# First FFN: one plain group instead of two in front of the groups of seven block products

## The chip, the cores and the metric

The kernel runs on one core of one Trainium2 chip. The metric is the device time of one execution in microseconds (us). Three runs of the kernel before gave 3054.82, 3054.83 and 3055.84 us, a median of 3054.83. The profiler's engines are PE (TensorE matmuls), PEld (TensorE's weight loads), DVE (VectorE), ACT (ScalarE), POOL (GpSimd) and SP (SyncE, which here only issues DMAs).

## The reference

The reference is a whole model on 512 rows of 1024 features: two layers of FFN, mixer, cross-attention and a second FFN, and then a hybrid block with an FFN of its own. Only the first operation of the first layer matters here:

```
def swiglu_ffn(x, w_gu, w_down):
    gate, up = jnp.split(x @ w_gu, 2, axis=-1)
    return (jax.nn.silu(gate) * up) @ w_down

x = x + 0.5 * swiglu_ffn(rms_norm(x, ffn1_norm[0]), ffn1_w_gu[0], ffn1_w_down[0])
```

The weight w_gu is 1024 x 5632 (gate and up of 2816 columns each), and everything is float32.

## The kernel before

Every float32 product is made of three matmuls on a split into an upper and a lower part: an operand `raw` becomes `wh` (rounded by ACT, line 100) and `wl` (the rest, subtracted by DVE, line 103), and TensorE adds wh·h, wl·h and wh·l (line 94). Weights stream from memory through four tiles `raw` (SP issues the loads), and each half megabyte of them is split by one ACT instruction of 128x1024 and then one DVE instruction of 128x1024. TensorE needs the lower part, so it waits for DVE.

The gate and up projection of an FFN is made in 11 groups of 256 gate columns and 256 up columns. There are two ways to make a group:

- **Plain.** Four chunks of 256 rows of the weight, for each of them 24 matmuls with 512 moving columns: 96 matmuls. Its inputs are the normed and split x (`hTh`, `hTl`), chunk by chunk.
- **Seven block products** (a fast matrix product: the weights and x are cut into two by two blocks). Seven times 24 matmuls with 256 moving columns: 168 matmuls. The seven blocks of weights have the names ge, s2, s1, s3, go, s4 and uo, in that order. Five of them are loads of half a megabyte by SP. s1 and s3 become sums while a second DMA, issued by POOL, adds to the tile; s2 and s4 are sums that DVE makes in a tile `u_raw`. On x's side the products need four sums of x's blocks, X1 to X4, each split into `u_Xnh` and `u_Xnl`.

The table `PLAIN` (line 246) says how many plain groups stand in front. In the last of them the sums of x are made ("builds" in `act_fast_up` and `dve_fast_up`). ACT multiplies x by the norm's gain into B, eight instructions of 128x512 on the tile `u_F` (`act_gained`). DVE combines blocks of B to X1, X2, X3 and X4 (`dve_combine`, four instructions of 128x1024). ACT rounds each of them to its upper part (`act_upper_x`), and DVE subtracts that for the lower part (`dve_lower_x`). The weights of the first group of seven are split by the same two engines, in program order among these:

```
                if builds and kp == 2:
                    dve_combine(dve, f, 4)
                    for i in X_ORDER[:2]:
                        dve_lower_x(dve, f, i)
                elif builds and kp == 3:
                    dve_split(dve, n + 4)
```

Here `dve_split(dve, n + 4)` makes the lower part of block ge, the first that TensorE needs of the group of seven; ahead of it DVE adds ge and s1 to s2 (`dve_lower_block`). ACT has the same order in `act_fast_up`: gains, upper X2 and X1, upper ge, upper X3 and X4, then the copy of the row scales (`u_R`).

In the first FFN ("f1u0" for its gate and up, line 860 for TensorE) the first plain group runs while x itself still arrives: TensorE transposes x between its matmuls, ACT and DVE split the transposed x straight out of the accumulator and copy it to `xT` (`act_start`, `dve_start`), ACT makes the row sums of squares, and POOL raises them to the power of -1/2 (`rc`, line 103). In the other four FFNs the plain groups start from an x that lies finished. POOL's own queue holds that power first and then the adding DMAs of s1 and s3 (`pool_fast_up`). All order is written out by hand: each engine works off its list, and a wait in the list holds what stands behind it.

Of the kernel before, what the change touches and what calls it, by code (L numbers as in the profile page):

```python
# [242 lines left out]
    return G  # L243


PLAIN = {"f1u0": 2, "f2u0": 1, "f1u1": 1, "f2u1": 1, "f3u": 2}
HALF = S // 2
BESIDE = {"in0": "out0", "in1": "out1", "gb": "yb"}

# [18 lines left out]
def program(nc, T, out):  # L268
# [80 lines left out]
    def fast(name, g):  # L349

        return g >= PLAIN.get(name, g + 1)

# [34 lines left out]
    def enter(e, key):  # L387
        for who in ("pe", "act", "dve", "pool"):
            e.wait_ge(ended, (key, who))
# [17 lines left out]
    def slot_of(name, g, what):  # L407

        r, odd = begin[name, PLAIN[name] - 1] % NRAW, (g - PLAIN[name]) % 2 == 0
        if what == "s1":  # L410
            return (raw[r], raw_in[r], s1_sum[0]) if odd else (more[0], more_in[0], s1_sum[1])
        if what == "s3":
            return (raw[(r + 2) % NRAW], raw_in[(r + 2) % NRAW], s3_sum[0]) if odd else (more[1], more_in[1], s3_sum[1])
        if what == "ge":
            return raw[(r + 1) % NRAW], raw_in[(r + 1) % NRAW], None
        if what == "go":
            return raw[(r + 3) % NRAW], raw_in[(r + 3) % NRAW], None
        return more[2], more_in[2], None
# [29 lines left out]
    def sp_weights(sp):  # L448
# [12 lines left out]
        for n, entry in enumerate(stream):  # L461
# [3 lines left out]
            if len(entry) == 3:  # L465
# [3 lines left out]
                for j, what, src in ((2, "s1", "ue"), (0, "ge", "ge"), (3, "s3", "ue"), (4, "go", "go"), (6, "uo", "uo")):  # L469
                    if (g, what) == (PLAIN[name], "uo"):  # L470
                        enter(sp, name)
# [53 lines left out]
    def dve_lower_block(dve, n):  # L525
        name, g, i = stream[n]
        block_ready(dve, name, g, i)
        if BLOCKS[i] == "ge":
            block_ready(dve, name, g, 2)
            s1 = slot_of(name, g, "s1")[0]  # L530
            if g > PLAIN[name]:
                dve.wait_ge(w_lo, n - 2)
# [1014 lines left out]
    class Ffn:  # L1547
        def __init__(self, up, down):
            self.up, self.down = up, down
            self.F, self.sg, self.R = Act(Fh, Fl, S, ("F", up)), u_sg, u_R  # L1550
            self.plain = PLAIN[up]

# [1795 lines left out]
```

How the kernel before makes its waits and increments, by code:

```python
    def wait_ge(self, flag, key):  # L75
        if self.e is None:
            return
        sem, value, who, place = flag.at[key]
        if who is not None:
            if self.seen.get(who, 0) >= place:
                return
            self.seen[who] = place
        else:
            if self.seen.get(sem, 0) >= value:
                return
            self.seen[sem] = value
        self.e.wait_ge(sem, value)
# [299 lines left out]
    def enter(e, key):  # L387
        for who in ("pe", "act", "dve", "pool"):
            e.wait_ge(ended, (key, who))
# [58 lines left out]
    def sp_weights(sp):  # L448
        sp.dma_start(x_rows[:, :, 0:256], x_in_rows[:, :, 0:256]).then_inc(x_in[0], 0, 16)
        first_weights(sp, 1)
        sp.dma_start(x_rows[:, :, 256:512], x_in_rows[:, :, 256:512]).then_inc(x_in[1], 0, 16)
        sp.wait_ge(x_in[0], 0)
        held = {}
        def load(tile, parts, flag_, key):
            for f_, k_ in held.get(tile, ()):
                sp.wait_ge(f_, k_)
            for dst, src in parts:
                sp.dma_start(dst, src).then_inc(flag_, key, 16)
# [31 lines left out]
    def act_first(act, kk):  # L491
        key = 0 if kk else "half"
        act.wait_ge(raw_in[0], key)
        act.activation(wh[0][:, kk, 0:chunk(0)], raw[0][:, kk, 0:chunk(0)], AF.Copy).then_inc(w_hi, key)
        act.split = 1
# [1 line left out]
    def dve_first(dve, kk):  # L497
        key = 0 if kk else "half"
        dve.wait_ge(raw_in[0], key)
        dve.wait_ge(w_hi, key)
# [248 lines left out]
    def act_square(act, N, src, c):  # L749
        act.wait_ge(x_ready, (src, c))
        if c >= 2:
```

## Time and profile before

| what | value |
|---|---|
| median of the runs | 3054.83 us |
| the profiled execution | 3054.1 us, its span 3052.4 us |
| TensorE busy | 3037.4 us, 17960 matmuls |
| VectorE busy | 2036.1 us |
| ScalarE busy | 1416.4 us |
| GpSimd busy | 450.5 us |
| mean granted TensorE clock | 0.999 |

A busy TensorE is a chain of pipelined matmuls: what one costs is read from the distance of two starts, not from its own duration. A granted clock of 1.00 is the level of 2.4 GHz and 0.50 that of 1.2 GHz. The first FFN's two plain groups stand before 55.11 us in the trace, its nine groups of seven behind that.

### The profile page before, as it was taken

How to read it: one execution, taken by the hardware profiler on the slowest of the kernel's cores; microseconds unless marked ns; L12 is line 12 of the kernel's file. 1: busy time of each engine (PE TensorE's matmuls, PEld its weight loads, DVE VectorE, ACT ScalarE, POOL GpSimd, SP SyncE). 2: the span in 40 equal slices, each digit the busy share in tenths (PEclk: the TensorE clock that was granted, in tenths of full speed). 3: DMA queues.
4: the chain of work that ended last, by engine and by line, in shares of the span. 5: the costliest groups of instructions: out<-in, count | busy, mean ns of one | idle time of the engine just before them, and what ended most of it. 6: DMA issues, size and time to landing. Idle time of an engine off the chain costs nothing.

```text
span 3052.4 us, 44801 instructions
## 1 busy us (share of the span) xinstructions
PE 3037.4 (100%) x17960; PEld 2620.2 (86%) x17960; DVE 2036.1 (67%) x2896; ACT 1416.4 (46%) x2189; POOL 450.5 (15%) x550
## 2 busy tenths in 40 slices
PE   9999999999999999999999999999999999999999
PEld 8998886887999899988867879998887786789987
DVE  7886258755888478863565657886336876578873
ACT  5444247544444244442455545444236727454442
POOL 1112014212110021100310212110153200031100
PEclk9999999999999999999999999999999999999999
DMA  7762330423874267633232416763332231247732
GB/s 209 176 165 98 103 97 29 148 67 99 198 176 136 97 160 176 166 107 104 83 99 75 152 49 165 177 167 106 89 96 83 82 105 35 76 111 190 170 117 70
DMA packets 287360, 366.93 MB, mean 120 GB/s; under 512 B 12304, under 2 KB 211344, under 8 KB 287024
## 3 DMA queue, kind: packets, MB, share of 16 engines
q1 hardware_dynamic: 233392, 304.42, 31.5%
q0 software_dynamic: 53184, 59.32, 12.0%
q8 instruction: 142, 2.33, 0.3%
q14 instruction: 66, 0.54, 0.1%
q10 hardware_dynamic: 576, 0.33, 0.0%
HBM read 361.92 MB, written 2.10 MB: 119 GB/s over the span
## 4 chain that ended last, share of the span: by engine, by line
PE 94%; issue 3%; DVE 2%; POOL 1%; ACT 0%; DMA 0%; POOLq 0%; ACTq 0%; DVEq 0%
PE ps L94 91%; PE ps L97 3%; POOL evQ L142 1%; DVE wl L103 0%; POOL evPb L142 0%; POOL evPa L142 0%; DVE hTl L109 0%; DMA misc<-in_misc 0%; DVE xT L103 0%; DVE u_X2l L103 0%; DVE u_raw L103 0%; DVE u_X3l L103 0%; DVE u_X4l L103 0%; DVE evQ L115 0%; DVE s_gb L103 0%
## 5 line engine op out<-in xcount | busy, mean ns | idle before, releaser
L103 DVE TENSOR_TENSOR wl<-raw,wh 128x1024 fp32r<-128x1024 f32 (+2 forms) x485 | 597.0, 1237 | 499.1 <-ACT wh L100 494.9
L100 ACT ACTIVATE wh<-raw 128x1024 fp32r<-128x1024 f32 (+2 forms) x485 | 505.1, 1049 | 810.9 <-PE ps L94 770.0
L94 PE MATMUL ps<-hTh,wh 128*128 128x256 f32 (+1 forms) x2016 | 671.0, 333 | 0.7 <-ACT hTh L100 0.7
L94 PE MATMUL ps<-hTh,wl 128*128 128x256 f32 (+1 forms) x2016 | 666.6, 331 | 0.0
L94 PE MATMUL ps<-hTl,wh 128*128 128x256 f32 (+1 forms) x2016 | 624.0, 330 | 0.2 <-DVE hTl L109 0.2
L94 PEld LDWEIGHTS ps<-hTh,wh 128*128 128x128 f32 x2016 | 383.9, 190 | 42.1 <-issue 9.2
L94 PEld LDWEIGHTS ps<-hTh,wl 128*128 128x128 f32 x2016 | 383.7, 190 | 37.7 <-issue 7.1
L94 PEld LDWEIGHTS ps<-hTl,wh 128*128 128x128 f32 x2016 | 382.1, 190 | 37.4 <-issue 4.7
L100 ACT ACTIVATE wh<-u_raw 128x1024 fp32r<-128x1024 f32 x190 | 201.4, 1062 | 297.8 <-PE ps L94 281.9
L94 PE MATMUL ps<-u_Fh,wl 128*128 128x512 f32 x704 | 273.9, 389 | 0.0
L94 PE MATMUL ps<-u_Fh,wh 128*128 128x512 f32 x704 | 273.9, 389 | 0.0
L103 DVE TENSOR_TENSOR wl<-u_raw,wh 128x1024 fp32r<-128x1024 f32 x190 | 232.2, 1222 | 40.1 <-ACT wh L100 39.7
L103 POOL TENSOR_TENSOR xn<-xn 128x512 f32<-128x512 f32 x69 | 100.1, 1450 | 988.8 <-ACT xn L100 751.4
L94 PE MATMUL ps<-u_Fl,wh 128*128 128x512 f32 x704 | 232.9, 389 | 0.0
L94 PE MATMUL ps<-wh,hTh 128*128 128x512 f32 (+2 forms) x576 | 216.8, 377 | 0.0
L94 PE MATMUL ps<-wl,hTh 128*128 128x512 f32 (+2 forms) x576 | 215.1, 374 | 0.0
L94 PE MATMUL ps<-wh,hTl 128*128 128x512 f32 (+2 forms) x576 | 195.1, 374 | 0.0
L94 PEld LDWEIGHTS ps<-u_Fl,wh 128*128 128x128 f32 x704 | 132.1, 188 | 27.5
L94 PEld LDWEIGHTS ps<-u_Fh,wl 128*128 128x128 f32 x704 | 132.2, 188 | 27.3
L94 PEld LDWEIGHTS ps<-u_Fh,wh 128*128 128x128 f32 x704 | 132.1, 188 | 27.3
L94 PEld LDWEIGHTS ps<-wh,hTh 128*128 128x128 f32 x576 | 108.3, 188 | 20.1 <-issue 2.2
L94 PEld LDWEIGHTS ps<-wl,hTh 128*128 128x128 f32 x576 | 108.4, 188 | 19.2 <-issue 1.4
(423 smaller groups left out, 6106.6 us busy)
## 6 DMA issues: line engine op xcount, KB each, us to landing
raw<-in_ffn_w_gu SPq DMA_DIRECT2D x118, 512.0 KB, 4.6
raw<-in_ffn_w_down SPq DMA_DIRECT2D x88, 512.0 KB, 3.6
u_raw<-in_ffn_w_gu SPq DMA_DIRECT2D x77, 512.0 KB, 4.9
raw<-in_ffn_w_gu POOLq DMA_DIRECT2D x40, 512.0 KB, 6.1
u_raw<-in_ffn_w_gu POOLq DMA_DIRECT2D x38, 512.0 KB, 6.1
raw<-in_xa_w_kv SPq DMA_DIRECT2D x32, 512.0 KB, 3.6
raw<-in_w_in SPq DMA_DIRECT2D x28, 512.0 KB, 3.6
raw<-in_od_w_in SPq DMA_DIRECT2D x24, 512.0 KB, 3.8
```

What stands on the lines that cost most here:

```text
L94: return self.made(lambda e: e.matmul(*a, **k))
L97: return self.made(lambda e: e.transpose(*a, **k))
L100: return self.made(lambda e: e.activation(*a, **k))
L103: return self.made(lambda e: e.tensor_tensor(*a, **k))
L142: return self.made(lambda e: e.affine_select(*a, **k))
```

## The change

One number: the first FFN gets one plain group, and then ten groups of seven.

```
-PLAIN = {"f1u0": 2, "f2u0": 1, "f1u1": 1, "f2u1": 1, "f3u": 2}
+PLAIN = {"f1u0": 1, "f2u0": 1, "f1u1": 1, "f2u1": 1, "f3u": 2}
```

So x's sums are made in the program's first group. On VectorE, right behind the split of the last plain chunk of that first group (`wl<-raw,wh` behind `rc<-stat`), stood before:

```order
L106 TENSOR_SCALAR rc<-stat 128x4
L103 TENSOR_TENSOR wl<-raw,wh 128x1024 x5
L103 TENSOR_TENSOR u_sg_63<-ps,u_R 128x512
L103 TENSOR_TENSOR u_sg_64<-ps,u_R 128x512
L103 TENSOR_TENSOR u_F<-ps,u_R 128x512 x2
L103 TENSOR_TENSOR u_F<-u_F 128x1024 x3
L103 TENSOR_TENSOR u_F<-u_F,u_sg_63 128x512
L103 TENSOR_TENSOR u_F<-u_F,u_sg_64 128x512
L103 TENSOR_TENSOR u_F<-u_F 128x1024
L103 TENSOR_TENSOR u_X2l<-u_F,u_X2h 128x1024
L103 TENSOR_TENSOR u_X1l<-u_F,u_X1h 128x1024
```

And now at the same place (`u_F<-u_F` are the four sums X1 to X4, `u_raw_60<-raw` is the weight sum s2, and the `wl` behind it is block ge):

```order
L106 TENSOR_SCALAR rc<-stat 128x4
L103 TENSOR_TENSOR wl<-raw,wh 128x1024
L103 TENSOR_TENSOR u_F<-u_F 128x1024 x4
L103 TENSOR_TENSOR u_X2l<-u_F,u_X2h 128x1024
L103 TENSOR_TENSOR u_X1l<-u_F,u_X1h 128x1024
L103 TENSOR_TENSOR u_raw_60<-raw 128x1024
L103 TENSOR_TENSOR wl<-raw,wh 128x1024
L103 TENSOR_TENSOR u_X3l<-u_F,u_X3h 128x1024
L103 TENSOR_TENSOR u_X4l<-u_F,u_X4h 128x1024
L103 TENSOR_TENSOR wl<-u_raw_60,wh 128x1024
```

Four splits of plain chunks are gone from between; the order from the sums of x to the split of ge is as it was.

On ScalarE, behind the copies of x (`xT<-ps`), stood before:

```order
L100 ACTIVATE xT<-ps 128x512 x4
L100 ACTIVATE wh<-raw 128x1024 x3
L100 ACTIVATE u_R<-ps 128x512
L100 ACTIVATE wh<-raw 128x1024
L100 ACTIVATE u_F<-xT,prm 128x512 x8
L100 ACT_TABLE_LOAD
```

And now:

```order
L100 ACTIVATE xT<-ps 128x512 x4
L100 ACTIVATE u_F<-xT,prm 128x512 x8
L100 ACTIVATE u_X2h<-u_F 128x1024
L100 ACTIVATE u_X1h<-u_F 128x1024
L100 ACTIVATE wh<-raw 128x1024
L100 ACTIVATE u_X3h<-u_F 128x1024
L100 ACTIVATE u_X4h<-u_F 128x1024
L100 ACTIVATE u_R<-ps 128x512
```

The eight gains follow the copies of x directly, and the copy of the row scales comes behind the upper parts of the sums.

## Rows read from the trace of the kernel before

**Rows 1.** The page: span, TensorE's busy time, the chain that ended last.

```profile
span 3052.4 us, 44801 instructions
PE 3037.4 (100%) x17960; PEld 2620.2 (86%) x17960; DVE 2036.1 (67%) x2896; ACT 1416.4 (46%) x2189; POOL 450.5 (15%) x550
...
PE 94%; issue 3%; DVE 2%; POOL 1%; ACT 0%; DMA 0%; POOLq 0%; ACTq 0%; DVEq 0%
```

**Rows 2.** Waits of TensorE over the span: us in total, times, longest.

```profile
PE ps L94 <- ACT evQ L100: 3.7, 3, 2.2
PE ps L94 <- POOL rc L103: 1.2, 1, 1.2
```

**Rows 3.** Windows: the second plain group, the first group of seven.

```profile
core 0: us, PE busy (x) PEld busy (x) DVE busy (x) ACT busy (x) POOL busy (x), PEclk, DMA share, GB/s
33.24:55.11 21.87, 21.87 (x99) 18.10 (x98) 19.74 (x21) 15.76 (x20) 3.51 (x3) 1.00 0.88 201
55.11:75.27 20.16, 20.16 (x170) 20.15 (x169) 16.77 (x19) 9.48 (x11) 2.55 (x2) 1.00 0.75 194
```

**Rows 4.** Timeline of PE: start, us, what; end of the first plain group.

```profile
32.43 1.05 PE L94 MATMUL ps<-misc,rc 128*128 128x128 f32 x8
33.24 0.48 PE L94 MATMUL ps<-hTh,wh 128*128 128x512 f32 x1
...
75.27 0.28 PE L94 MATMUL ps<-hTh,wh 128*128 128x256 f32 x1
75.39 0.28 PE L94 MATMUL ps<-hTh,wl 128*128 128x256 f32 x1
```

**Rows 5.** Timeline of ACT: copies of x, plain splits, gains, upper parts.

```profile
24.61 2.04 ACT L100 ACTIVATE xT<-ps 128x512 f32<-128x512 f32 x4
26.51 2.97 ACT L100 ACTIVATE wh<-raw 128x1024 fp32r<-128x1024 f32 x3
33.60 0.60 ACT L100 ACTIVATE u_R<-ps 128x512 f32<-128x512 f32 x1 [4.11 <-PE ps L94]
...
35.04 5.01 ACT L100 ACTIVATE u_F<-xT,prm 128x512 f32<-128x512 f32 x8
...
42.42 1.04 ACT L100 ACTIVATE u_X2h<-u_F 128x1024 fp32r<-128x1024 f32 x1
```

**Rows 6.** Timeline of DVE: last split of group one, sums, block ge.

```profile
24.80 1.22 DVE L103 TENSOR_TENSOR wl<-raw,wh 128x1024 fp32r<-128x1024 f32 x1 [0.85 <-ACT wh L100]
...
45.85 1.22 DVE L103 TENSOR_TENSOR u_X1l<-u_F,u_X1h 128x1024 fp32r<-128x1024 f32 x1
46.98 1.22 DVE L103 TENSOR_TENSOR u_raw<-raw 128x1024 f32<-128x1024 f32 x1
48.12 1.22 DVE L103 TENSOR_TENSOR wl<-raw,wh 128x1024 fp32r<-128x1024 f32 x1
...
53.79 1.28 DVE L103 TENSOR_TENSOR u_sg<-ps,u_R 128x512 f32<-128x512 f32 x2
```

**Rows 7.** Timeline of POOL, and landings of its two first adding DMAs.

```profile
24.11 1.02 POOL L103 TENSOR_TENSOR rc<-rc,half 128x4 f32<-128x4 f32 x1 [23.06 <-DVE rc L106]
...
raw<-in_ffn_w_gu POOLq DMA_DIRECT2D x1, 512.0 KB, 7.6
...
raw<-in_ffn_w_gu POOLq DMA_DIRECT2D x1, 512.0 KB, 10.3
```

**Rows 8.** Windows around TensorE's longest pause: PEclk is the granted clock.

```profile
482.75:484.75 2.00, 0.00 (x0) 0.00 (x0) 0.14 (x1) 2.00 (x6) 0.55 (x2) 1.00 0.00 0
...
485.50:485.75 0.25, 0.25 (x4) 0.13 (x2) 0.00 (x0) 0.25 (x1) 0.00 (x0) 0.55 0.00 0
485.75:488.50 2.75, 2.75 (x13) 1.85 (x9) 2.31 (x2) 2.56 (x8) 1.17 (x1) 0.50 0.00 0
...
488.75:489.00 0.25, 0.25 (x2) 0.25 (x4) 0.25 (x1) 0.25 (x2) 0.25 (x1) 0.62 0.68 49
489.00:490.00 1.00, 1.00 (x7) 0.53 (x6) 0.81 (x2) 0.55 (x3) 1.00 (x3) 1.00 0.79 305
```

**Rows 9.** Timeline of PE behind that pause, at the lower clock.

```profile
484.86 1.46 PE L94 MATMUL ps<-e_kbT,e_qbT 64*128 64x384 f32 x8 [2.17 <-ACT evQ L100]
...
487.59 0.63 PE L94 MATMUL ps<-hTh,wl 128*128 128x512 f32 x1
488.01 0.63 PE L94 MATMUL ps<-hTh,wh 128*128 128x512 f32 x1
```

**Rows 10.** Windows at the program's end, where TensorE stops.

```profile
3046.00:3047.00 1.00, 0.94 (x5) 0.44 (x3) 1.00 (x2) 0.03 (x1) 0.00 (x0) 1.00 0.08 27
...
3049.00:3050.00 1.00, 0.00 (x0) 0.00 (x0) 0.93 (x2) 0.00 (x0) 0.00 (x0) 0.50 0.00 0
```

## The prediction

> **What bounds the kernel now.** I read the page first, then the waits of TensorE, then the windows and the engines' timelines from 20 to 80 us. On the page TensorE is busy in 3037.4 of 3052.4 us and makes up 94% of the chain that ended last [rows 1]. Its longest wait in the whole span is 2.2 us [rows 2]. So the time is the sum of what TensorE does, and each us in which it is made to wait is a us of the result, unless it was waiting later anyway. DVE is the second engine: it is busy for 19.74 of the 21.87 us of the second plain group, where x's sums are made, and for 16.77 of 20.16 us in a group of seven [rows 3].
>
> **What goes: TensorE's work.** The second plain group runs from 33.24 to 55.11 us, which is 21.87 us; a group of seven runs from 55.11 to 75.27 us, which is 20.16 us [rows 3]. Neither holds a gap. One plain group less and one group of seven more takes 21.87 - 20.16 = 1.71 us away, if the new group can start at 33.24 us, where the transposed scales of the first group are done and the next group begins now [rows 4]. At both bounds this term is the same, since both durations stand in the trace.
>
> **What the new group waits for.** Its first product needs x itself, which is long split, and the lower part of block ge. DVE comes to that split only behind the sums, and these wait for ACT's eight gains.
>
> - ACT ends its copies of x at 24.61 + 2.04 = 26.65 us [rows 5]. What follows now, three plain splits, is gone, so the gains start there. They take 5.01 us for eight, the last ends at about 31.7 us. The gains can't go earlier: the copies they read end at 26.65, and ACT has no idle time in front.
> - DVE has split the last plain chunk at 24.80 + 1.22 = 26.0 us [rows 6] and then waits for B. X1 needs only the first four gains (about 29.2 us) and is out of the way. X2 needs the last gain and starts at 31.75.
> - From X2 to the lower part of ge DVE has seven instructions of 128x1024 in a row: X2, X3, X4, the lower X2, the lower X1, the sum s2, and ge's lower part. Such instructions start 1.14 us apart and the last takes 1.22 us [rows 6], so 6 x 1.14 + 1.22 = 8.06 us: ge is ready at 39.8 us. ACT's upper X2 and X1 (1.04 us each [rows 5], from about 33.0) and upper ge are done by 36 us, ahead of DVE.
> - TensorE therefore stands from 33.24 to 39.8 us: a new wait of **6.55 us**. The second plain group was the cover for this chain; now nothing but the first group's end stands beside it.
>
> Bounds of this term: if X2 waited for nothing and the gains were free, DVE would still need 8.06 us from 26.0 us for the seven and 1.14 for X1, and ge would be ready at 35.2 us, a wait of 2.0 us. If all of DVE's instructions took the 1.22 us of a single one [rows 6], it is 7.1 us. I take 6.55, which follows the order as it stands.
>
> **The second wait.** Behind ge DVE has the lower X3, the lower X4 and s2's lower part: 3 x 1.14 us more, done at 43.2 us. Block ge's product of 24 matmuls takes 24 x 0.12 = 2.88 us (starts 0.12 us apart [rows 4]) and ends at 42.7. So 0.5 us more are lost. From there DVE is ahead: s1 at 44.3, s3 at 46.7 (with two evictions of 0.6 us [rows 6] in between), against starts of TensorE at 46.1 and 49.0; uo at 55.0 against 57.6. At TensorE's next group it is 2.5 us ahead, and behind that the pattern is the one of now.
>
> **What stands at nothing.** SP issues five loads of 512 KB in place of eight of 256 KB, and POOL two adding DMAs more, 1.5 MB in all. SP's first two (s1, ge) go out when the tiles of the first chunks come free, at the same places as the plain loads now. POOL's s1 stands behind the power, which ends at 24.11 + 1.02 = 25.1 us; the two first adding DMAs landed 7.6 and 10.3 us after issue [rows 7], so s1 lands at 32.7 to 35.4 us, and DVE asks for it with s2's sum at 37.4. It is hidden by two to five us, but only by the wait itself: each us that the chain of sums lost would bring it nearer. The copy of the row scales, now behind ACT's upper parts, falls to about 38 us, and its first reader on DVE is at 44.3. The last group of seven gets one multiplication of 128x1024 by the row scales more on DVE, about 1.2 us, inside the 20.16 - 16.77 = 3.4 us that DVE has free there [rows 3]; without that cover it would be 1.2 us.
>
> **The clock.** In the row TensorE stood still from 482.75 to 484.75 us, and from 485.5 to 488.8 us the granted clock was 0.50, the 1.2 GHz level, though TensorE was working again [rows 8]. At the end of the program it stops within 3046 to 3047 us and the clock is at 0.50 by 3049 [rows 10]. A pause of 6.55 us is over three times the one and longer than the other, so I expect the clock to be at 0.50 when the new group starts. Two matmuls of 512 columns lay 0.42 us apart at the lower level [rows 9], so 256 columns lie about 0.21 apart by halving, against 0.12 now. If the low stretch again lasts 3.3 us, it costs 3.3 x (1 - 0.12 / 0.21) = 1.4 us. It falls into block ge's product, behind which TensorE would have waited 0.5 us anyway, so 0.9 us remain. Bounds: 0 if the clock is back in time, and a stretch twice as long costs 2.8 - 0.5 = 2.3 us.
>
> The Trainium skill has the rule for this on "TensorE: Matmul & The Clock Gate", section "What's actually happening": the throttled state is the default, and only activity lifts it. By that rule the pause is paid twice, as a wait and as slow matmuls behind it, and the sum below is 6.3 us; without it 5.4 us. The stretch at 0.50 in the trace agrees with it.
>
> **The sum.** 6.55 + 0.5 + 0.9 - 1.71 = +6.3 us, rounded. Against the profiled execution of 3054.1 us that is 3060.4. The median of the runs shown lies 0.7 above that execution, so a median of the changed kernel should be near 3054.8 + 6.3 = 3061.1 us. TensorE is the chain's owner all the way behind, so I see nothing that pays it back.
>
> **Rivals.**
>
> - *The clock holds.* The pause is paid once: 6.55 + 0.5 - 1.71 = 5.4 us, 3060.2. For it: in the trace the clock fell only 0.7 us after TensorE had started again (484.86 us [rows 9]), so when it falls and when it comes back is not fixed to the pause. Against it: both pauses of the trace led to 0.50. Chance 0.15.
> - *The low clock lasts twice as long*, or a term of the chain grows as much (an adding DMA of s1 beyond its 10.3 us by over 2 us): 5.4 + 2.3 = 7.7 us, 3062.5. For it: nothing in the trace says how soon the clock comes back behind a longer pause, and there is one stretch alone to measure by. Chance 0.14.
> - *The time comes back later.* The other engines gain 6 us of lead while TensorE stands, and waits like the 3.7 us on evQ [rows 2] shrink: 6.3 - 3.7 = 2.6 us, 3057.4. Against it: that wait is for ACT's work on what TensorE has just made, so it moves along. Chance 0.05.
> - *Faster.* The sums of x stay covered: TensorE starts the new group at 33.24 us, or before 33.24 + 1.71 = 34.95, from which on it is a loss. Then the gain of 1.71 us is left, 3053.1. The place is DVE's split of ge: it would have to be done 4.8 us earlier than worked out. That takes gains that run beside x's copies, or a split of ge ahead of the sums, and the written order has neither. Chance 0.03.
>
> **How the numbers follow.** The forecast, +5.8 to +7.0 us with its own range of 3060 to 3062, has a chance of 0.63. About 0.2% (6.1 us) is what a measurement of this kernel can tell from no change, and the forecast lies on that line: of its 0.63 I give 0.40 to the upper side and 0.23 to the lower. Slower by over 0.2%: 0.40 + 0.14 = 0.54, and 0.01 of the clock's rival by the spread of the runs: 0.55. Within 0.2%: 0.23 + 0.14 + 0.05 = 0.42. Faster: 0.03. The range takes in the first two rivals with the runs' spread: from 3054.1 + 4.9 = 3059.0 to 3054.8 + 8.2 = 3063.0.
>
> **What would show it.** In the profile after: TensorE's last row of the first group at about 33.2 us, and its first matmul of 256 columns at 39.8, with the wait put down to DVE's wl. The four `u_F<-u_F` rows of DVE from 29 to 35 us, and ge's wl ending at 39.8. PEclk at 0.50 in some 3 us from about 39 us on, and the first 24 matmuls of 256 columns 0.2 us apart for a while. TensorE's second group of seven beginning at about 61.4 us in place of 55.11, and from there the same distance to the end. The prediction is wrong if 256-column matmuls start before 35 us, if ge's split on DVE stands in front of the sums, or if the distance at 61 us is not the one at the end.

## The result, and the profile after

The changed kernel takes 3061.22 us (median of 14 runs, 3060.80 to 3062.89) against 3054.90 us (14 runs, 3054.29 to 3056.79): 6.3 us more, a ratio of 1.0021 with a 95% interval of 1.0014 to 1.0029. The forecast was 3061.1. The profiled execution took 3062.45 us, 1.2 us over its median, and that of the kernel before 3054.1 us, 0.8 us under its own; so the two profiles lie 8.3 us apart, more than the medians.

The page of the changed kernel, for [rows 1]:

```profile
span 3060.7 us, 44966 instructions
PE 3038.6 (99%) x18032; PEld 2625.0 (86%) x18032; DVE 2045.7 (67%) x2905; ACT 1420.8 (46%) x2193; POOL 452.5 (15%) x552
```

TensorE has 72 matmuls more (168 - 96) and is busy for only 1.2 us more, although the span grew by 8.3 us. The difference is waiting, and the waits of TensorE name it at once (total, times, longest). Of [rows 2] nothing grew by more than 0.3 us; one row is new, with a wait of 6.1 us in the first group and one of 0.44 us far behind, at 1117.49 us, to which I come back:

```profile
PE ps L94 <- DVE wl L103: 6.5, 2, 6.1
PE ps L94 <- ACT evQ L100: 4.0, 4, 2.2
PE ps L94 <- POOL rc L103: 1.2, 1, 1.2
```

Timeline of PE at the end of the first group, which answers to [rows 4]: start, us, what, and the idle time in front with its releaser. From the second fence line on the matmuls are those of the new group of seven.

```profile
32.99 1.05 PE L94 MATMUL ps<-misc,rc 128*128 128x128 f32 x8
40.13 0.58 PE L94 MATMUL ps<-hTh,wh 128*128 128x256 f32 x1 [6.09 <-DVE wl L103]
40.51 0.41 PE L94 MATMUL ps<-hTh,wl 128*128 128x256 f32 x1
40.73 0.41 PE L94 MATMUL ps<-hTl,wh 128*128 128x256 f32 x1
...
45.42 0.32 PE L94 MATMUL ps<-u_X2h,wh 128*128 128x256 f32 x1
...
46.05 0.28 PE L94 MATMUL ps<-u_X2l,wh 128*128 128x256 f32 x1
46.17 0.28 PE L94 MATMUL ps<-u_X2h,wh 128*128 128x256 f32 x1
...
62.72 0.28 PE L94 MATMUL ps<-hTh,wh 128*128 128x256 f32 x1
```

Block ge's 24 matmuls start 0.21 us apart (5.29 us in all), block s2's 0.12 us apart, and the next group begins at 62.72 us. The first group itself began some 0.5 us later in this profile than in that of before; it does so in every later profile but four, three of which are of the changed kernel itself (32.43 to 32.51 us), so it is no part of the change. From here on I measure from the transposition of the scales (the row of `misc,rc`): to the next group it was 55.11 - 32.43 = 22.68 us before and is 62.72 - 32.99 = 29.73 us now.

The two engines behind the wait, first ACT, then DVE (for [rows 5] and [rows 6]):

```profile
24.92 2.04 ACT L100 ACTIVATE xT<-ps 128x512 f32<-128x512 f32 x4
26.99 5.02 ACT L100 ACTIVATE u_F<-xT,prm 128x512 f32<-128x512 f32 x8
```

```profile
25.11 1.23 DVE L103 TENSOR_TENSOR wl<-raw,wh 128x1024 fp32r<-128x1024 f32 x1 [0.85 <-ACT wh L100]
29.68 1.23 DVE L103 TENSOR_TENSOR u_F<-u_F 128x1024 f32<-128x1024 f32 x1 [3.35 <-ACT u_F L100]
32.04 3.50 DVE L103 TENSOR_TENSOR u_F<-u_F 128x1024 f32<-128x1024 f32 x3 [1.13 <-ACT u_F L100]
35.46 1.22 DVE L103 TENSOR_TENSOR u_X2l<-u_F,u_X2h 128x1024 fp32r<-128x1024 f32 x1
36.59 1.22 DVE L103 TENSOR_TENSOR u_X1l<-u_F,u_X1h 128x1024 fp32r<-128x1024 f32 x1
37.73 1.22 DVE L103 TENSOR_TENSOR u_raw<-raw 128x1024 f32<-128x1024 f32 x1
38.86 1.22 DVE L103 TENSOR_TENSOR wl<-raw,wh 128x1024 fp32r<-128x1024 f32 x1
```

Read it from below: ge's lower part ends at 38.86 + 1.22 = 40.08 us and TensorE starts at 40.13. Above it DVE goes without a gap back to 32.04, and there it waited 1.13 us for ACT's last gain; in front of X1 it had waited 3.35 us for the first gains.

The clock (windows; the third last number is the granted clock, the columns are those of [rows 3]), for [rows 8]: 0.50 is already there in the pause, and for all of block ge.

```profile
33.80:38.50 4.70, 0.24 (x3) 0.05 (x1) 4.70 (x5) 4.70 (x6) 0.00 (x0) 1.00 1.16 255
39.00:40.13 1.13, 0.00 (x0) 0.00 (x0) 1.13 (x2) 1.13 (x2) 0.45 (x1) 0.50 0.00 1
40.13:45.42 5.29, 5.29 (x25) 5.29 (x25) 5.29 (x6) 3.25 (x4) 0.83 (x1) 0.50 0.77 164
45.50:62.72 17.22, 17.22 (x145) 17.22 (x145) 16.71 (x20) 8.25 (x10) 2.55 (x2) 1.00 0.84 222
```

### The profile page after: what moved, and what is told of

It reads as the page before. It is cut to its first block, busy times and chain, and to the rows that moved or that the text cites. A ratio compares the mean times of both kernels' runs of the same rounds, so it can differ in the third digit from the quotient of the medians.

```text
span 3060.7 us, 44966 instructions
## 1 busy us (share of the span) xinstructions
PE 3038.6 (99%) x18032; PEld 2625.0 (86%) x18032; DVE 2045.7 (67%) x2905; ACT 1420.8 (46%) x2193; POOL 452.5 (15%) x552
## 4 chain that ended last, share of the span: by engine, by line
PE 93%; issue 3%; DVE 2%; POOL 1%; ACT 1%; DMA 0%; POOLq 0%; ACTq 0%; DVEq 0%
PE ps L94 90%; PE ps L97 3%; POOL evQ L142 0%; DVE wl L103 0%; POOL evPb L142 0%; DVE u_F L103 0%; DMA misc<-in_misc 0%; ACT u_F L100 0%; DVE u_raw L103 0%; DVE u_X2l L103 0%; DVE hTl L109 0%; POOL evPa L142 0%; DVE xT L103 0%; DVE u_X4l L103 0%; DVE u_X3l L103 0%
```

## The experiments

Each kernel was compared with the kernel before on the same chip; medians of before in these comparisons were 3054.85 to 3055.02 us (for x9_look and x10_look there is one run of before, 3053.57 us).

**1. TensorE kept busy in the pause (x1_warm).** Added to the changed kernel, behind the first plain group:

```
...
+            if (g, kp) == (0, None):
+                b = home["f1u0", 1] + 1
+                pe.wait_ge(drained, pe.held[b])
+                pe_warm(pe, b, 30)
```

> The changed kernel with 30 dummy products of 128 columns (on the constant `ones`, into an accumulator bank that is free) behind the first plain group, so that TensorE works through the new wait instead of standing. Theory: the wait for DVE stays (first matmul of 256 columns at 39.8 to 40.1 us), but the granted clock stays at 1.00; block ge takes 2.9 us in place of 5.3, 0.5 us of wait for s2 come back, and the group of seven from its first matmul to the next group's takes about 20.7 us in place of 22.6. Time 3060.2 us, 1 to 2 us under the changed kernel. Rival, that the slow block is not the pause's doing but that of DVE's lower parts coming late: the group still takes 22.6 us and the time stays at 3061.2.

Measured: 3060.36 us (11 runs, 3059.95 to 3061.25). Windows of the dummy products and of the group of seven:

```profile
34.10:40.70 6.60, 6.60 (x62) 6.60 (x61) 6.60 (x7) 6.25 (x8) 0.92 (x1) 1.00 0.85 191
40.72:61.16 20.44, 20.44 (x172) 20.29 (x170) 20.41 (x24) 11.11 (x13) 1.61 (x2) 1.00 0.83 198
```

The clock stays at 1.00, the group takes 20.44 us in place of 62.72 - 40.13 = 22.59, and with the dummies it lasts 27.95 us from the transposition to the next group. The dummies ran 0.4 us beyond what was needed (ge was ready at 40.3). So the pause has a price of its own for the wait, and a second one for the clock. On the way to the next group, the overrun included, the second is 29.73 - 27.95 = 1.8 us against the result's profile and 1.0 to 1.2 us against the two shorter profiles of experiment 7. In the medians it is 0.9 us: nine of these eleven runs lie under the lowest of the changed kernel's, 3060.80 us.

**2. The sums without the gains (x2_nogain).** The first FFN's sums are taken from x; the eight gains and the wait for them are gone, so the norm's gain is missing in the sums.

```
...
-            return Bf[:, 4 * k:4 * k + 4, HALF * t:HALF * t + HALF]
+            return (xT if f.up == "f1u0" else Bf)[:, 4 * k:4 * k + 4, HALF * t:HALF * t + HALF]
...
```

> The changed kernel without the eight gains of the first FFN: x's sums are taken from x itself (the norm's gain is left out of the sums). Theory: the sums start when x's last copy is there, 27.0 us in place of 32.0, and ge is ready after eight DVE instructions, 36.2 to 36.6 us; s2's sum asks for s1's adding DMA at about 33.8, which lands at about 34.2. TensorE's wait falls from 6.3 to about 2.5 us, and the time to about 3057 us with the clock at 1.00 and 3058 if it still falls. Rival, that the gains run beside what DVE would wait for anyway (s1's sum): the wait stays above 5 us, the time above 3060.

Measured: 3056.90 us (11 runs, 3056.06 to 3059.45); the profiled execution took 3057.79 us. DVE and PE:

```profile
27.34 1.23 DVE L103 TENSOR_TENSOR u_F<-xT 128x1024 f32<-128x1024 f32 x1 [0.70 <-ACT xT L100]
...
35.53 1.22 DVE L103 TENSOR_TENSOR wl<-raw,wh 128x1024 fp32r<-128x1024 f32 x1
...
36.80 0.39 PE L94 MATMUL ps<-hTh,wh 128*128 128x256 f32 x1 [2.49 <-DVE wl L103]
```

The wait falls from 6.09 to 2.49 us. So the gains are 3.6 us of it, and the other 2.5 us are DVE's eight instructions. In the profiled execution the clock still fell, but late (windows behind the restart); its mean over the span is 0.999 there, while six of the other ten runs, the median among them, show 1.000.

```profile
36.80:38.00 1.20, 1.20 (x10) 1.20 (x11) 1.20 (x2) 0.85 (x1) 0.00 (x0) 1.00 1.19 242
38.50:41.50 3.00, 3.00 (x16) 3.00 (x16) 3.00 (x4) 2.34 (x2) 1.28 (x1) 0.50 1.07 367
42.00:43.00 1.00, 1.00 (x11) 1.00 (x10) 1.00 (x2) 1.00 (x2) 0.21 (x1) 1.00 0.99 110
```

**3. Block ge's split first (x4_ge_first).** The changed kernel with another order only. DVE's list (ACT's follows it; X4 goes into the group of seven):

```
...
+                    dve_combine(dve, f, 1)
+                    dve_combine(dve, f, 2)
+                    dve_split(dve, n + 4)      # ge
+                    dve_lower_x(dve, f, 2)
+                    dve_first_sum(dve)         # s2's sum
+                    dve_lower_x(dve, f, 1)
+                    dve_split(dve, n + 5)      # s2
+                    dve_split(dve, n + 6)      # s1
+                    dve_combine(dve, f, 3)
+                    dve_split(dve, n + 7)      # s3
+                    dve_lower_x(dve, f, 3)
...
```

> The changed kernel with another order in its first group: ACT rounds block ge right behind the gains, DVE makes ge's lower part right behind X2 and then each lower part when TensorE needs it (X2, s2's sum, X1, s2, s1, X3, s3, X3; X4 only in the group of seven). Nothing is added or left out. Theory that the place of ge's split makes the wait, and DVE's amount of work the rest: ge is ready at 34.4 us and the first wait is 0.6 us, but DVE is busy without a gap from 32 to 57 us and TensorE waits for it in several pieces of under 2.2 us, about 4 us in all; next group's first matmul at 57.6 to 58.5 us; the clock stays up; 3057.4 us. Rival, that the order is the whole cause: waits under 1 us in all and 3054 us. Rival, that the amount alone decides: the next group at 61 us, 3060.

Measured: 3058.83 us (11 runs, 3058.34 to 3060.38), 1.4 us over the theory's number. All of TensorE's new waits in the stretch and the next group:

```profile
33.17 1.05 PE L94 MATMUL ps<-misc,rc 128*128 128x128 f32 x8
34.65 0.39 PE L94 MATMUL ps<-hTh,wh 128*128 128x256 f32 x1 [0.43 <-DVE wl L103]
39.48 0.39 PE L94 MATMUL ps<-u_X2h,wh 128*128 128x256 f32 x1 [1.69 <-DVE wl L103]
...
48.83 0.39 PE L94 MATMUL ps<-hTh,wh 128*128 128x256 f32 x1 [0.45 <-DVE wl L103]
52.46 0.36 PE L94 MATMUL ps<-hTh,wh 128*128 128x256 f32 x1 [0.50 <-DVE u_F L103]
56.46 0.35 PE L94 MATMUL ps<-u_X4h,wh 128*128 128x256 f32 x1 [0.91 <-DVE u_X4l L103]
...
59.41 0.28 PE L94 MATMUL ps<-hTh,wh 128*128 128x256 f32 x1
```

The first wait is 0.4 us (0.6 worked out), and 4.0 us of waits in five pieces stand in the stretch. From the transposition to the next group it takes 26.24 us: half of the 7.0 us come back. The pieces are short and the clock stayed at 1.00 in all of the stretch. So neither rival holds: the old order costs about 3.5 us, clock included, and the rest is DVE's work behind the gains (it is busy for 25.26 of the 25.43 us from 33.98 to 59.41 us), which this order does not take away. The number was too low, partly because each short wait also costs some 0.1 to 0.3 us until matmuls are 0.12 us apart again: 26.24 us are 5.3 us more than 0.81 us of transposition and a group of 20.16 us, and only 4.0 of them are counted as waits.

**4. One plain group more where x lies finished (x3_f2u0_two).** In the kernel before, `"f2u0": 2` in place of 1.

> The kernel before with two plain groups in place of one in the second FFN of the first layer, where x lies finished when the first group begins. Theory that a plain group costs 21.87 and a group of seven 20.16 us and that the sums are covered by one plain group there: 1.7 us longer, 3056.6 us, no new wait in the trace. Rival, that one plain group is too short a cover there too: faster than before.

Measured: 3055.90 us (11 runs, 3055.38 to 3056.71), 1.0 us more, less than expected and within the spread of the runs (ratio 1.0002, 0.9993 to 1.0011); so it is the trace that has to tell. In that kernel's trace the added plain group begins at 760.76, the first group of seven at 782.64 and the next at 802.79:

```profile
760.76 0.48 PE L94 MATMUL ps<-hTh,wh 128*128 128x512 f32 x1
...
782.64 0.28 PE L94 MATMUL ps<-hTh,wh 128*128 128x256 f32 x1
...
802.79 0.28 PE L94 MATMUL ps<-hTh,wh 128*128 128x256 f32 x1
```

21.88 and 20.15 us: the price of a plain group is as read. But in the kernel before, behind one plain group, that first group of seven runs from 760.68 to 781.26 us, 20.58 us. So one plain group is just too short a cover there, by 0.4 us, and the gain of one plain group less is 1.3 us in that FFN. The rival was right in a small part: even with a finished x the cover is used up.

**5. The first group rearranged (x5_filled).** As experiment 3, and in addition: the last four copies of x go from ACT to DVE, ACT's gains follow some 1 us earlier (26.11 us in place of 26.99), behind ge's upper part, s1's adding DMA stands in front of the power, and DVE's list begins with s2's sum and ge:

```
...
+        for c in range(4, KD):
+            keep(c)
...
+                    dve_first_sum(dve)
+                    dve_split(dve, n + 4)
+                    dve_combine(dve, f, 1)
+                    dve_combine(dve, f, 2)
+                    dve_split(dve, n + 5)
...
+        pool_sums_of_weights(pool, "f1u0", 1, "s1")
         pool_power(pool, "f1u0")
...
```

> The changed kernel with its first group rearranged, nothing added or left out. DVE makes the four late copies of x that ACT made, in a stretch where DVE had nothing to do, so ACT's gains start 2 us earlier; POOL issues the adding DMA of s1 in front of the power; ACT rounds block ge in front of the gains, and DVE makes s2's sum and ge's lower part while it waits for the gains; the rest as in the run before with ge's split first. Theory that TensorE waits because DVE's work from the last gain on is too much, so that work moved into DVE's free time in front of it comes straight off: the first wait is gone, what is left is under 2 us in pieces, the next group begins 22.0 to 23.5 us behind the scales' transposition (before: 22.7; changed: 29.7; ge first: 26.2), and the time is 3054.0 to 3055.5 us, the kernel before within 1 us. Rival, that the earlier adding DMA and the copies collide with the start (TensorE's first group gets longer): over 3056 us.

Measured: 3055.19 us (11 runs, 3054.64 to 3056.75; ratio 1.0001, 0.9992 to 1.0009). DVE's work moved to the front, and the waits left in the stretch:

```profile
21.85 2.47 DVE L121 COPY xT<-ps 128x512 f32<-128x512 f32 x4
...
26.68 1.23 DVE L103 TENSOR_TENSOR u_raw<-raw 128x1024 f32<-128x1024 f32 x1
27.82 1.22 DVE L103 TENSOR_TENSOR wl<-raw,wh 128x1024 fp32r<-128x1024 f32 x1
```

```profile
33.24 1.05 PE L94 MATMUL ps<-misc,rc 128*128 128x128 f32 x8
48.97 0.35 PE L94 MATMUL ps<-hTh,wh 128*128 128x256 f32 x1 [0.28 <-DVE u_F L103]
52.97 0.36 PE L94 MATMUL ps<-u_X4h,wh 128*128 128x256 f32 x1 [0.91 <-DVE u_X4l L103]
...
55.91 0.28 PE L94 MATMUL ps<-hTh,wh 128*128 128x256 f32 x1
```

22.67 us to the next group, before's 22.68. DVE has the same instructions and four copies more. The copies now stand in 2.4 us of its idle time in front of the rows shown for the changed kernel, and s2's sum and ge's lower part in the 3.35 us that DVE waited for the first gains. The 6.3 us are back. The four moves were made together, so what each of them is worth alone is not shown.

**6. The first group's products later (x7_products_late).** Experiment 5, with the two products of the first plain group's gate and up behind the split of the next group's ge:

```
...
+                if (f.up, g, i) == ("f1u0", 1, 4):
+                    plain_product(0, 0)
+                    plain_product(0, 1)
```

> The rearranged first group of the run before (x5_filled), with the two products of the first plain group's gate and up (two DVE instructions, 1.28 us) behind the split of the next group's ge instead of behind the third block. Theory that DVE's amount of work in front of a block sets what is left of the waits: the two waits of TensorE left there (0.3 us for a sum of the left half, 0.9 us for the lower X4) fall under 0.2 us in all, the next group begins 21.2 to 21.8 us behind the scales' transposition (22.67 with x5_filled, 22.68 before), and the time is 0.9 to 1.5 us under x5_filled: 3053.8 to 3054.3 us. Rival: the waits move into the second group of seven, 22.7 us up to there and 3055.2.

Measured: 3053.77 us (11 runs, 3052.78 to 3055.68) against 3054.85 (15 runs); the ratio of 0.9997 has an interval from 0.9988 to 1.0006. TensorE:

```profile
32.53 1.05 PE L94 MATMUL ps<-misc,rc 128*128 128x128 f32 x8
51.08 0.36 PE L94 MATMUL ps<-u_X4h,wh 128*128 128x256 f32 x1 [0.23 <-DVE u_X4l L103]
54.03 0.28 PE L94 MATMUL ps<-hTh,wh 128*128 128x256 f32 x1
```

21.50 us, 1.18 under before: of the 1.71 us of TensorE's work that much is now a gain. In the medians it is 1.1 us, which is within the spread of the runs; the trace shows it, the times alone don't prove it.

**7. The changed kernel again (x6_again, x8_look, x9_look, x10_look).** No edit.

> The changed kernel as it is, once more. In its first profile the granted clock was 0.50 for 5.3 us of TensorE's work behind the pause, in place of the 3.3 us of the prediction, and four of its 14 runs were 1.4 us over the other ten. Theory that the stretch at the lower clock has two lengths from run to run: most runs at 3061.0 to 3061.5, and a profile of such a run shows the lower clock for 1.5 to 3.5 us of TensorE's work and the next group 28 us behind the scales' transposition; a run at 3062.5 shows 29.7 again. Rival, that the length is fixed by the pause: 5.3 us and 29.7 us whatever the time.

> The changed kernel as it is, one profile more, for a run of its shorter kind. Theory of two lengths: if the profiled run is at 3061.0 to 3061.5, the lower clock lies on 1.5 to 3.5 us of TensorE's work behind the pause and the next group begins about 28.5 us behind the scales' transposition; at over 3062 it is 5.3 us and 30 us again. Rival: 30 us at either time.

> The changed kernel as it is, another profile. All three profiles so far were of runs at 3062.2 to 3062.7 us, and all have a second stretch at the lower clock, 3.4 us long at 493 us, as the kernel before has at 486 us in its profile. Theory that the 1.4 us between the two kinds of runs is this second stretch: a run at about 3061 shows none there, and behind the first pause the same 5.3 us as ever (next group 29.7 to 30.5 us behind the scales' transposition). Rival, that the first stretch is shorter in such runs: 28.5 us there.

> As x9_look, once more: the same two theories, 29.7 to 30.5 us and no second stretch at 493 us in a run at 3061 us, or 28.5 us.

Measured: x6_again 3061.89 us (10 runs, 3060.96 to 3063.09; ratio 1.0022, 1.0013 to 1.0031). The profiled runs, with that of the result: "at 0.50" is the part of block ge's product with the clock at 0.50, "to next" the way from the transposition to the next group, and "second" says whether there is another stretch at 0.50 at about 493 us, where TensorE waits 2.2 us for evQ.

| profiled run | us | wait for ge | block ge | at 0.50 | to next | second |
|---|---|---|---|---|---|---|
| result | 3062.45 | 6.1 | 5.29 | all | 29.73 | yes |
| x6_again | 3062.23 | 6.5 | 5.28 | all | 30.07 | yes |
| x8_look | 3062.67 | 6.8 | 5.28 | all | 30.48 | yes |
| x9_look | 3060.23 | 6.1 | 4.50 | 3.5 us | 28.95 | no |
| x10_look | 3061.06 | 6.1 | 4.75 | 4.1 us | 29.16 | no |

Windows of x9_look:

```profile
33.28:36.00 2.72, 0.24 (x3) 0.05 (x1) 2.72 (x3) 2.72 (x4) 0.00 (x0) 1.00 1.18 237
36.50:39.50 3.00, 0.00 (x0) 0.00 (x0) 3.00 (x3) 2.65 (x5) 0.42 (x1) 0.50 0.64 174
39.64:43.00 3.36, 3.36 (x15) 3.36 (x16) 3.36 (x4) 3.08 (x3) 0.72 (x1) 0.50 0.61 125
43.50:61.42 17.92, 17.92 (x151) 17.92 (x150) 17.89 (x22) 8.49 (x10) 2.06 (x2) 1.00 0.86 216
```

Both theories of the difference are true in part. In the two shorter profiles the clock falls earlier in the pause and comes back earlier, and block ge takes 4.50 and 4.75 us in place of 5.28: 0.5 to 0.8 us. From the next group to the end of the span they take 2997.1 and 2997.2 us, the longer three 2997.9 to 2998.0: another 0.7 to 0.9 us, with the second stretch in the longer three alone. Together that is the 1.4 us between the two kinds of runs. (The longer waits for ge in x6_again and x8_look are no mark of a kind: the result's profile has the short one.) Both shorter profiles come from one chip, so the profiles alone don't tell the chip from the kind; but the ten runs of x6_again, of both kinds, all come from one chip.

## Why the prediction was right

- **What goes.** 21.87 - 20.16 us per group: confirmed by experiment 4 (21.88 and 20.15 us), and 1.18 of the 1.71 us appear as a gain once the waits are gone (experiment 6).
- **The wait for ge, 6.55 us.** From the end of the first group to the first matmul it is 40.13 - 33.80 = 6.33 us in the result's profile (the trace counts 6.09, from the recorded end of the last matmul) and 6.7 us in x6_again, whose first group starts as before's did; ge was ready at 40.08 and 39.90 us against 39.8 worked out. The parts are right too: gains to 32.0 us, X2 behind the last of them, seven instructions 1.14 us apart. Experiment 2 gives the gains 3.6 us of it. The lower bound of that term (2.0 us without the gains) measured 36.80 - 34.07 = 2.7 us counted the same way, since X1 starts 0.7 us later there: it must wait for the last copy of x and not for DVE's last split.
- **The second wait, 0.5 us.** It is there only when the clock stays up: 43.78 us is s2's first matmul in x1_warm, in step with DVE's lower part of s2; 0.2 us of it are left there, since the dummies let ge start 0.4 us late. In the changed kernel the slow block covers it, as the prediction said.
- **The clock, 0.9 us net.** The mechanism was right, the term is mis-sized. The low stretch is 6.8 us long in place of the 3.3 of [rows 8], but 1.4 to 3.3 us of it lie in the pause, where they cost nothing; 3.5 to 5.3 us fall on TensorE's work. Against a block of 2.88 us and 0.5 us of wait, ge's 4.50 to 5.29 us are 1.1 to 1.9 us net. A rival had the low clock "twice as long" at 2.3 us: the result lies between it and the forecast, nearer to the forecast in the shorter runs. What the Trainium skill says on "TensorE: Matmul & The Clock Gate", section "What's actually happening" (the throttled state is the default and activity lifts it), agrees: x1_warm's dummy products held 1.00 through the same pause.
- **The sum.** From the transposition to the next group the change adds 6.3 to 7.8 us (28.95 to 30.48 against 22.68), worked out 6.3; the medians differ by 6.3. By the parts it is 6.36 + 0.5 + 1.12 - 1.71 = 6.27 us in x9_look and 6.33 + 0.5 + 1.91 - 1.71 = 7.03 us in the result's profile. That the forecast and the medians agree to a tenth is partly luck: the terms add up to 6.24 us and were rounded up to 6.3, the clock term was some 0.2 to 1.0 us low, and the profile of before from which I summed has a second stretch at 0.50 and a mean granted clock of 0.999, while many of its runs show 1.000, as if without that stretch (of those only the clock was looked at).
- **What lies behind.** The prediction saw the pattern of before from the second group of seven on, and named another distance at the end as a sign of being wrong. Between the two profiles the distance is 62.72 - 55.11 = 7.6 us at that group and 8.3 us at the end. So 0.7 us more arise behind it: nearly 0.4 us between 492 and 502 us, where a new wait of 0.24 us on evQ stands at 496.74 us, and some 0.3 us at 1117.49 us, where TensorE waits for the lower part of s2 in the second layer's first FFN. This wait of 0.44 us is in all five profiles of the changed kernel, in x1_warm and in x4_ge_first, and not in those of before, x2_nogain, x3_f2u0_two, x5_filled and x7_products_late. Why an edit of the first FFN brings it is open. The profiles of x9_look and x10_look, which have it too but no second stretch at 0.50, take as long behind that group as before's, 2997.1 and 2997.2 against 2997.3 us.
- **What stood at nothing.** s1's adding DMA was issued at 25.39 and landed 8.8 us later, at 34.2; DVE asked for it at 37.73. It was hidden with 3.5 us to spare. In x2_nogain that cover shrinks: the sum starts 0.1 us behind DVE's turn.
- **The rivals.** "The clock holds" was made on purpose by x1_warm and measured 3060.4 (worked out 3060.2). "The time comes back later" did not happen: the wait on evQ was 3.8 to 4.4 us in all the profiles from the change on, 3.7 before. "Faster" needed gains beside x's copies or ge in front of the sums; experiments 5 and 6 put ge in front, and 6 is the one kernel with a median below before's, by 1.1 us, within the spread.

## What to carry to other kernels

A step that is hidden behind work has two sizes: how long it takes, and when its first input is there. When its cover is cut, redo the sum from the last input to the first reader through the in-order list of the busiest engine, not from busy shares. When a wait remains after reordering, look for the idle time of that engine in front of the wait and move independent work into it; here that gave back all 6 us, while reordering alone gave 3.5 of the 7.0 us of the stretch. TensorE's pauses of 6.1 us and more were paid twice in all five profiles of the changed kernel, as a wait and as slower matmuls behind it; price both, and let cheap dummy products separate the two.

## What was not expected of the hardware

In these profiles the clock's low stretch came in two lengths: 3.3 to 3.4 us (at 486 to 496 us, behind a pause of 2.2 us, and in x2_nogain behind one of 2.5 us) and 6.8 us (behind the pauses of 6.1 to 6.8 us). It began in the pause, 3 to 6 us after TensorE stopped (x9_look: 36.3 us, x8_look: 38.9 us), or only after the restart (x2_nogain: at about 38.3 us, 1.5 us after it). The same pause of 2.2 us on evQ was followed by a low stretch in the profiles of before, the result, x2_nogain, x6_again and x8_look, and by none in x1_warm, x3_f2u0_two, x4_ge_first, x5_filled, x7_products_late, x9_look and x10_look. Where the long stretch lies and whether the short one comes changes from run to run of the same kernel and moves its time by about 1.4 us, nearly as much as the 1.71 us of work that the change takes away.

Two kernels whose pauses in the first group were of up to 1.7 us (x4_ge_first, x5_filled) kept 1.00 there.
